# First layer of a two-block network: the gates' pair of column blocks placed directly behind queries and keys, the value block and the turned probabilities behind it

## The reference

```python
hn = rmsnorm(x, norm_g)
proj = hn @ w_in
q, k, v, u, z_a, z_b = jnp.split(proj, cuts, axis=-1)
o_a = chunked_relpos_attention(q.reshape(shp), k.reshape(shp), v.reshape(shp), rel_bias)
o_a = o_a * jax.nn.silu(z_a)
y = jax.nn.gelu(s5_ssm(u, lam_re, lam_im, log_dt, b_re, b_im, c_re, c_im, d_skip).astype(x.dtype))
o_b = y * jax.nn.sigmoid(y @ w_glu + b_glu)
o_b = o_b * jax.nn.silu(z_b)
return x + jnp.concatenate([o_a, o_b], axis=-1) @ w_out
```

## Time and profile before

| | us |
|---|---|
| median of 3 runs | 2536.39 |
| lowest, highest | 2535.34, 4633.48 |
| profiled execution | 2535.48 |
| its span (first to last instruction) | 2533.8 |
| one turn of the first layer (start of the product of u to the next) | 44.24 |

### The profile page before, as it was taken

One profiled execution on the slowest core, in us unless ns is written; L12 is line 12 of the kernel. 1 busy time (PEld: TensorE's weight loads), 2 busy tenths in 40 slices (PEclk: granted clock), 3 DMA queues, 4 the chain that ended last, 5 costly groups with the idle time before them and its releaser, 6 DMA issues.

```text
span 2533.8 us, 60188 instructions
## 1 busy us (share of the span) xinstructions
PE 2515.1 (99%) x23116; PEld 2456.7 (97%) x23116; DVE 1784.5 (70%) x3601; ACT 658.1 (26%) x1663; POOL 435.3 (17%) x576
## 2 busy tenths in 40 slices
PE   9999999999999999999999999999999999999998
PEld 8999999999999999999999999999999999999997
DVE  8888876565565556799989977555555656777854
ACT  4334321110011112243343331221220012344311
POOL 2434330010010000244434411121120000000000
PEclk9999999999999999999999999999999999999999
DMA  7344434444444444434343444343334444444443
GB/s 266 134 159 157 164 134 167 170 154 162 170 166 153 157 166 167 157 143 159 139 166 141 186 161 171 126 156 134 134 134 167 166 166 172 160 151 188 158 167 116
DMA packets 65834, 403.04 MB, mean 159 GB/s; under 512 B 6832, under 2 KB 15424, under 8 KB 19648
## 3 DMA queue, kind: packets, MB, share of 16 engines
q1 hardware_dynamic: 65056, 399.46, 42.5%
q0 software_dynamic: 672, 2.11, 0.5%
HBM read 399.43 MB, written 2.11 MB: 158 GB/s over the span
## 4 chain that ended last, share of the span: by engine, by line
PE 98%; DVE 1%; ACT 0%; issue 0%; DMA 0%; DVEq 0%; SPq 0%; ACTq 0%
PE psum L667 80%; PE psum L613 3%; PE psum L604 2%; PE psum L1189 1%; PE psum L848 1%; PE psum L642 1%; PE psum L750 1%; PE psum L1198 1%; PE psum L964 1%; PE psum L635 1%; PE psum L1151 1%; PE psum L743 0%; PE psum L773 0%; PE psum L786 0%; PE psum L1130 0%; PE psum L932 0%
## 5 line engine op out<-in xcount | busy, mean ns | idle before, releaser
L667 PE MATMUL psum<-h,ring 128*128 128x128 f32 x4978 | 598.5, 275 | 0.3 <-ACT probT L1258 0.3
L667 PEld LDWEIGHTS psum<-h,ring 128*128 128x128 f32 x4978 | 575.9, 192 | 4.9 <-ACT vN L1386 2.7
L667 PE MATMUL psum<-mix,ring 128*128 128x128 f32 x4122 | 492.0, 275 | 0.0
L667 PEld LDWEIGHTS psum<-mix,ring 128*128 128x128 f32 x4122 | 476.0, 192 | 0.3 <-DVE near L2000 0.2
L2007 DVE TENSOR_TENSOR near<-psum,near 128x128 f32<-128x128 f32 x162 | 46.9, 289 | 345.6 <-PE psum L667 345.5
L1967 DVE TENSOR_TENSOR ring<-ring 128x1024 f32<-128x1024 f32 x130 | 163.5, 1258 | 0.0
L667 PE MATMUL psum<-ring,h 128*128 128x128 f32 x1296 | 153.7, 275 | 0.0
L667 PEld LDWEIGHTS psum<-ring,h 128*128 128x128 f32 x1296 | 149.1, 192 | 0.0
L2000 DVE TENSOR_TENSOR near<-psum,near 128x128 f32<-128x128 f32 x162 | 46.8, 289 | 143.8 <-PE psum L667 139.6
L1258 ACT ACTIVATE w<-psum 128x128 f32<-128x128 f32 x75 | 20.8, 277 | 467.9 <-PE psum L667 467.9
L1966 DVE TENSOR_TENSOR ring<-ring 128x1024 f32<-128x1024 f32 x101 | 129.6, 1283 | 5.0 <-DMA ring<-w_out 3.9
(11 more groups left out here) (541 smaller groups left out, 4370.5 us busy)
## 6 DMA issues: line engine op xcount, KB each, us to landing
ring<-w_out SPq DMA_DIRECT2D x80, 1024.0 KB, 5.0
ring<-w_odd SPq DMA_DIRECT2D x64, 1024.0 KB, 4.9
ring<-w_hgrn SPq DMA_DIRECT2D x64, 1024.0 KB, 5.5
ring<-w_nsa SPq DMA_DIRECT2D x48, 1024.0 KB, 5.8
ring<-w_even SPq DMA_DIRECT2D x40, 1024.0 KB, 5.6
ring<-w_rg SPq DMA_DIRECT2D x40, 1024.0 KB, 5.3
mix<-w_even SPq DMA_DIRECT2D x8, 1024.0 KB, 4.8
ring<-w_cmp_in SPq DMA_DIRECT2D x8, 1024.0 KB, 6.0
```

Source lines behind the costliest of these rows:

```text
L667: mm = pe.matmul(dst, stationary, moving, start=new and j == 0, stop=new and j == kh - 1, skip_group_check=not new)
```

## The change

In a turn PE now does the gates' pair directly behind queries and keys. The scores stand behind unit 2 of the gates, the value block behind unit 7, and the two heads' turned probabilities at the end of the turn. The pairs' units are numbered 2 to 8 and 9 to 15, the value block is 16. ACT copies `vN` and `probT` at the end of a turn, behind `rotations`; PE's wait for `vN` moves to the next user of bank 0. On DVE, in turns 1 to 7, `three_forms` of the gates stands directly behind `two_sums` of queries and keys, and the fourth and fifth sum stand before the second group's scan and rotate. In turn 0 DVE's list stays as it is. SP's list keeps its order, but the value tile's fill now waits for the last unit of the turn before.

```diff
--- before.py
+++ after.py
@@ -252,9 +252,9 @@
 
 
         even1 = Phase(PAIRS, 16, [Load(0, tiles("w_even1", 0), SLOT, 1), Load(1, tiles("w_even1", 1), SLOT, 7),
-                                  Load(2, tiles("w_even1", 2), SLOT, 8), Load(11, tiles("w_even1", 3), SLOT, 9),
-                                  Load(6, None, 0, 16, 2), Load(3, tiles("w_even1", 4), SLOT, 15),
-                                  Load(4, tiles("w_even1", 5), SLOT, 16)], (5,))
+                                  Load(2, tiles("w_even1", 2), SLOT, 8), Load(11, tiles("w_even1", 3), SLOT, 16),
+                                  Load(6, None, 0, 16, 2), Load(3, tiles("w_even1", 4), SLOT, 14),
+                                  Load(4, tiles("w_even1", 5), SLOT, 15)], (5,))
         glu = Phase(1, 8, [Load(n, tiles("w_glu", n), SLOT, 2 * n + 2) for n in range(4)])
 
         def four(name, slots):
@@ -294,7 +294,7 @@
 
         for f in (fast1, fast2, fast_h, fast_c, fast_nsa, fast_odd, fast3, fast_rg, fast4):
             f.first += EVEN
-        fast_e = Fast(even1, ((1, 2, None), (5, 6, None)), 8, 0, True, 1, 1)
+        fast_e = Fast(even1, ((1, 2, None), (5, 6, None)), 8, 0, True, 1)
         mix_flat = mix[:, :, :].rearrange("p k t -> p (k t)")
         wides = [w[:, :, :].rearrange("p k t -> p (k t)") for w in (wide_a, wide_b, wide_c)]
         h_flat = h[:, :, :].rearrange("p k t -> p (k t)")
@@ -826,18 +826,18 @@
 
             def values_and_gates(i):
 
-                pe.wait_ge(first_read, after(2 * fast_e.number(i, 1)))
+                block_products(fast_e, i, 1, of_h, sums_even, 4, None, (), ((2, lambda: scores(i)),))
+                pe.wait_ge(first_read, after(2 * fast_e.number(i, 2)))
                 values(even1, i, 3, bank[0])
-                scores(i)
-                pe.wait_ge(v_ready, after(i + 1))
-                block_products(fast_e, i, 1, of_h, sums_even, 4, None, (),
-                               ((5, lambda: (turn_head(i, 0), turn_head(i, 1))),))
+                for e in range(2):
+                    turn_head(i, e)
 
             def even_turn(i):
 
                 pe.wait_ge(bu_used, after(4 * i))
                 product(even1, i, 0, bank[4])
                 mix_values(i - 1)
+                pe.wait_ge(v_ready, after(i))
                 block_products(fast_e, i, 0, of_h, sums_even, 4, None, (),
                                ((1, lambda: read_outs(i - 1)), (2, lambda: drives(i))))
                 values_and_gates(i)
@@ -862,6 +862,7 @@
             last = PAIRS - 1
             pe.wait_ge(y_mixed, after(last))
             pe.wait_ge(first_read, after(2 * EVEN))
+            pe.wait_ge(v_ready, after(PAIRS))
             wait_load(pe, glu, 0, 0)
             glu_block(0, 0, 7)
             mix_values(last)
@@ -1382,8 +1383,6 @@
                     first_reads(fast_e, i, 0, q_and_k, None, lambda: gelu(i - 1))
                 if not last:
                     angles(i + 1)
-                s.wait_ge(used, done(even1, i, 9))
-                s.activation(vN[:, :], bank[0][:, 0:T], ACT.Copy).then_inc(v_ready, 1)
 
                 def softmax():
 
@@ -1398,9 +1397,6 @@
                         ins.then_inc(p_ready, 1)
 
                 first_reads(fast_e, i, 1, z_in, None, softmax)
-                for e in range(2):
-                    s.wait_ge(pt_ready, after(2 * i + e + 1))
-                    s.activation(probT[:, e, :], bank[HEAD_BANKS[e]][:, 0:384], ACT.Copy).then_inc(pt_used, 1)
                 z_pair = fast_e.number(i, 1)
                 s.wait_ge(first_read, after(2 * z_pair + 2))
                 s.wait_ge(later_read, after(5 * z_pair + 5))
@@ -1411,6 +1407,12 @@
                 s.activation(sq[:, 0, :], z_in[:, 1, :], ACT.Tanh, scale=0.5).then_inc(zb_tanh, 1)
                 if not last:
                     rotations(i + 1)
+                s.wait_ge(o_ready, after(i))
+                s.wait_ge(used, done(even1, i, 16))
+                s.activation(vN[:, :], bank[0][:, 0:T], ACT.Copy).then_inc(v_ready, 1)
+                for e in range(2):
+                    s.wait_ge(pt_ready, after(2 * i + e + 1))
+                    s.activation(probT[:, e, :], bank[HEAD_BANKS[e]][:, 0:384], ACT.Copy).then_inc(pt_used, 1)
                 st.leave(PAIRS - 2 if not first and not last else 1)
 
             s.wait_ge(con_in, 16)
@@ -2286,18 +2288,18 @@
                 scan(0)
                 if not first:
                     two_sums(fast_e, i, 0, q_and_k)
+                    three_forms(fast_e, i, 1)
                 rotate(i, 0)
                 drive(i, 1)
                 if first:
                     first_raw(1, 8, later_read, 5)
                     v.sem_inc(forms_made, 2)
                     three_forms(fast_e, i, 1)
-                scan(1)
-                rotate(i, 1)
                 if not first:
                     fourth_sum(fast_e, i, 0, q_and_k)
                     fifth_sum(fast_e, i, 0, q_and_k)
-                    three_forms(fast_e, i, 1)
+                scan(1)
+                rotate(i, 1)
                 fourth_form(fast_e, i, 1)
                 drive(i, 2)
                 maxima(i)
```

## The result

The changed kernel takes 2580.01 us in the median of four runs (2578.42 to 2581.37), the kernel before 2535.9 beside it: a ratio of 1.0174 [1.0161, 1.0187]. The profiled execution took 2578.99 us, its span 2577.3. The forecast was 2575 with a range of 2562 to 2587.

| stretch | before | after | difference | forecast |
|---|---|---|---|---|
| start to the first product of turn 1 | 58.38 | 66.30 | +7.9 | +7.4 |
| turns 1 to 7, up to the first product behind them | 309.7 | 345.6 | +35.9 | +30.9 |
| the rest | 2165.7 | 2165.4 | -0.3 | 0 |

The account below looks back on a forecast made before the run. PE was taken to bound every turn. Seven turns 30.7 us, turn 0 7.4 and the last turn's end 0.2 make 38.3 on 2535.48: 2573.8, as median 2575; range 2562 to 2587, the forecast's own 2568 to 2584.

Parts of the forecast that it names:

- What bounds the kernel: First layer's turns: PE, busy in all of 44.24 us, bounds each; waits added to PE lengthen the kernel in full.
- The chain on DVE: DVE from queries' and keys' two sums to the gates' first sum, counted from 120.35 to 135.95 in the new order.
- The case in which DVE pays in the fourth form: Fourth form beside POOL's second state: if DVE were slowed, some 0.4 us a turn more, 2578 us.
- The release of 0.37 us: Time from the end of DVE's or ACT's work to PE's start, taken as 0.37 us, read behind vN.
- the gain of 0.2 us from vN: Between scores and gates: PE's wait for vN goes, giving between 0 and 0.33 us a turn, taken as 0.2.
- the two waits: New PE waits each turn: 1.3 us ahead of the gates' unit 2, 3.3 us ahead of unit 4, together 4.58.
- The clock rival: PE's clock falls in the new gaps, some 1.9 us per restart; 2577 if in turn 0 alone, 2590 if every turn; 10%.
- Turn 0: DVE's list unchanged; PE waits 4.5 us ahead of unit 2 and 3.1 us ahead of unit 4, less 0.2: 7.4 us.
- SP's queue: The value tile's later fill delays slot 6 and the gates' tiles, but they land in time: no cost.
- the 1.2 us behind its start that were counted: ACT's three end-of-turn copies, behind the rotations, were to follow 1.2 us into the 7 us product of u: no cost.

Follow-up runs that it names:

- PE's order alone: PE's, ACT's and SP's new order, with DVE keeping the order of the kernel before: 2591.66 us, ratio 1.0219 to the kernel before.
- the second profile: The changed kernel run and profiled once more, unaltered: 2579.66 us, ratio 1.0171 to the kernel before; its profiled execution took 2581.8 us.
- DVE's order alone: The kernel before with only DVE's new order, PE, ACT and SP as before: 2535.27 us, ratio 0.9998 to the kernel before.

## Why the prediction was nearly right

- **What bounds the kernel** held. PE had no idle time to give, each new wait came through in full, and the place is the one named: 48.52 us in a turn where 48.6 was expected, behind the fourth sum and behind line 2002.
- **The chain on DVE** was right to 0.1 us. The turn of the forecast began at 102.63, the turn shown at 117.61. The fourth sum's end was put 25.57 us into it and came at 25.52, the first sum's 33.32 and came at 33.41. The forms took 139.45 - 135.91 = 3.54 us. The reason given, that POOL has nothing to do beside them, held. The case in which DVE pays in the fourth form didn't come: beside it POOL took 1.65 us, in place of the 0.73 of the same line for the first group (at 140.90), and DVE 1.22. The Trainium skill (GPSIMD Engine Reference, the table at its head, "SBUF interfaces") names the two as sharing an interface, and both this and the 1.74 us in PE's order alone agree with it; here it was once POOL alone that paid, and once both (POOL's operation took 1.71 us there).
- **The release of 0.37 us failed.** It is 0.05 (143.13 to 143.18, 151.02 to 151.07). The 0.37 between vN's end and unit 1 wasn't a release: from the scores' start to the unit is 0.86 us before and after (145.16 to 146.02), with and without vN. PE was still at the scores, so the gain of 0.2 us from vN was nothing either. By starts unit 2 is late by 143.18 - (140.49 + 1.79) = 0.90 us and not 1.27, unit 4 by 151.07 - (146.02 + 1.79) = 3.26 and not 3.31. That makes 4.16 of the turn's 4.28. The other 0.12 is the balance of small shifts from one start to the next: the two units behind a wait take 1.98 and 1.89 us in place of 1.79 (0.29 more), the gates' unit 1, which stood behind the scores, 1.79 in place of 1.89, and the value block 7.15 in place of 7.24. That 48.52 came so near to 48.6 is in part luck: the two waits were put 0.42 us too long, mainly for the release, and against that stand the 0.2 for vN and these 0.12 that nothing was put down for. Six turns at 4.28 and the last, with the layer's end, at 4.20 are 29.9 us in place of 30.9.
- **The clock rival came true in part**, and it is the step by which the forecast was short: 6.1 us in the first profile, 9.2 in the second. It had 10% for one fall a turn at 1.9 us each. What came is a fall in three to five of seven turns, of 1.4 to 2.9 us each. That the time stayed inside the range is due to the room above the forecast and not to a price for this. The argument against it was only that the trace of before never stands still so long; that says nothing of what happens once it does. The Trainium skill (TensorE: Matmul & The Clock Gate, "HAM oscillation — how this bites in real kernels") has the clock throttled again when PE idles for some microseconds between bursts; the traces agree for waits of 4.6 us, each of them in turns 1 to 7 followed by a fall in the one profile, agree for only some of those of 3.0, and show none behind those of up to 1.4. In turn 0 the fall that the rival priced at 1.9 us cost nothing: the scores are over at 48.22, DVE's maxima begin at 49.30 without a wait for them, the first sum is over at 51.12, and PE waits 1.07 us in spite of the fall.
- **Turn 0** gave 7.9 us with what lies ahead of it, for 7.4. Unit 1 began 1.54 us later than in the earlier trace rows, but DVE's forms only 0.76 (40.07 for 39.31), and the end of the turn goes by DVE: its first sum is over 0.76 us later than in the earlier trace rows, PE is released 0.15 us behind it in place of 0.37, and 7.4 + 0.76 - 0.22 is the 7.9. In the second profile of the same kernel unit 1 began at 36.98 and the forms at 39.66, 0.35 us later than in the earlier trace rows, and turn 1 began 7.5 us later than before. The start itself belongs to the run and not to the change: PE's product of line 642, ahead of everything that was changed, began at 16.42 for 14.88 in the first profile and at 14.99 in the second, and with DVE's order alone, which leaves turn 0 as it was, turn 1 began 1.0 us later than in the trace of before.
- **SP's queue** cost nothing, as forecast. POOL, which masks the bias when slot 6 has landed, started 6.1 us into the turn, and no form waited for a transfer. The rest of the span gave -0.3 us, for which no cause was looked for.

Sum: the forecast's 2573.8 for the profiled execution, 1.0 less for the turns, 6.1 more for the clock, 0.5 more for turn 0 and 0.3 less for the rest, makes 2579.1; it took 2578.99.

```profile
123.73 0.19 POOL L1762 COPY cur<-s 128x8 f32 x1 [11.01 <-DMA ring<-rel]
```

```profile
117.56 0.36 ACT L1412 ACTIVATE vN<-psum 128x256 f32<-128x256 f32 x1
```

The two rows are POOL's, behind its wait for slot 6 of 11.01 us, at 123.73 (117.61 + 6.1), and ACT's copy of vN, 0.05 us ahead of the next turn's product of u, earlier than the 1.2 us behind its start that were counted, and without cost.

## What to carry to other kernels

Where one engine is busy throughout, ask of a block that is moved what it was covering: here 7.24 us of products hid 4.2 us of another engine's list, and when it went, all of that came through. The second engine's list must be reordered with the first's, each producer ahead of what nobody waits for, and the next holder of the same bank on the third engine too: such moves, of forms, sums and one copy, brought the 56 us of PE's order alone down to 1.6. Where a change leaves PE idle for some 3 us, price the slow restart at its full worth and not as a tail, and look whether a second wait behind it hides it.

## What the runs showed of the hardware

- From DVE's or ACT's end to PE's start it is 0.05 to 0.06 us behind the sums and ACT's copy in turns 1 to 7, 0.13 behind the forms in PE's order alone (145.28 + 1.23, PE at 146.64), and 0.05 and 0.15 in turn 0. An apparent release of 0.37 was PE finishing its own work.
- With the same waits on PE (3.0 us in turns 1 to 6, 2.76 in turn 7) the granted clock fell in three turns of seven in one execution and in five in another. In the one profile with waits of 4.5 to 4.6 us it fell in each of the seven; in none of the six kernels whose waits were 1.4 us or less in turns 1 to 7 did it fall there. In turn 0, behind waits of 3.3 to 4.4 us, unit 2 took 2.9 to 3.8 us in six of seven profiles and 2.05 in one.
- Eight useless products in the idle time made the kernel 7 us faster, without moving the end of the wait.
- A fall of the clock can reach the critical path by way of another engine: DVE waited 1.53 us for scores that a slow PE had made late.
- What decides in which turn a wait of 3.0 us costs a fall stays open: turns 1, 4 and 6 fell in both executions, 2 and 7 in one, and no run here varied when in the turn the wait comes.
